# The first tile's k and q units on x times the norm's weights, its root multiplied in where the banks are emptied

## What is computed

```python
h = x * rsqrt(mean(x * x) + 1e-6) * g_pre_mix
z, q, k, v, glow, og = split(h @ w_in)
gk = log_sigmoid(glow @ w_gk2 + b_gk2) / 16
pool_out = pool_mixer(z)                 # causal window means, a map per group
gla_out  = gla_mixer(q, k, v, gk, og)    # gated linear attention, 4 heads
x = x + rmsnorm(concat(pool_out, gla_out) @ w_o)
x = x + rmsnorm(conv_ffn(rmsnorm(x)))
x = x + (p @ w_ple) * sigmoid(x @ w_ple_gate)
```

## Time and profile before

| | us |
|---|---|
| runs of the kernel before | 2514.07 (median), 2513.3, 2518.11 |
| the profiled execution, its own time | 2515.29 |
| its span, first to last instruction | 2513.5 |
| PE busy in the span | 2492.4 (99%) |
| DVE busy | 1542.4 (61%) |
| ACT busy | 1256.4 (50%) |
| POOL busy | 178.5 (7%) |
| mean granted clock of TensorE, share of full | 0.999 |

### The profile page before, as it was taken

The page is one execution under the profiler, slowest core; times in us unless marked ns, Lnnn a source line. Parts: engine busy times, 40 slices in busy tenths (PEclk is TensorE's granted clock), DMA queues, the critical chain, the costliest instruction groups (busy, mean ns, idle before and its releaser), DMA issues.

```text
span 2513.5 us, 40470 instructions
## 1 busy us (share of the span) xinstructions
PE 2492.4 (99%) x16216; PEld 2429.2 (97%) x16216; DVE 1542.4 (61%) x2479; ACT 1256.4 (50%) x1959; POOL 178.5 (7%) x508
## 2 busy tenths in 40 slices
PE   9999999999999999999999999999999999999999
PEld 8889999989999999999999999999999999999999
DVE  7668765556665554666545466654546664647865
ACT  5455554554444455544445544444545444546554
POOL 4201000100000010000001000000100000010000
PEclk9999999999999999999999999999999999999999
DMA  8555556554444656444465644446564444676665
GB/s 252 181 187 160 183 147 224 195 200 147 151 122 129 217 178 209 151 152 126 125 221 175 214 151 151 123 126 212 177 217 151 144 125 128 206 251 208 192 184 170
DMA packets 128250, 437.40 MB, mean 174 GB/s; under 512 B 13760, under 2 KB 23360, under 8 KB 127552
## 3 DMA queue, kind: packets, MB, share of 16 engines
q1 hardware_dynamic: 128064, 434.82, 54.2%
HBM read 403.48 MB, written 31.28 MB: 173 GB/s over the span
## 4 chain that ended last, share of the span: by engine, by line
PE 95%; DVE 2%; DMA 1%; ACT 1%; issue 0%; POOL 0%; SPq 0%; DVEq 0%; POOLq 0%; ACTq 0%
PE G L1682 29%; PE G L1683 28%; PE G L1684 28%; PE X L1728 2%; PE G L1966 1%; PE G L1967 1%; PE G L1968 1%; PE X L1786 1%; PE X L1678 1%; DMA kept_lo<-w_lo 1%; DVE w_lo L1164 0%; DMA stage<-in_w_up_units_dram 0%; PE X L1792 0%; PE X L1707 0%; PE X L1771 0%
## 5 line engine op out<-in xcount | busy, mean ns | idle before, releaser
L1682 PE MATMUL G<-h_hi,w_hi 128*128 128x384 f32 (+2 forms) x3072 | 997.9, 325 | 6.5 <-DVE w_lo L1164 3.3
L1683 PE MATMUL G<-h_hi,w_lo 128*128 128x384 f32 (+2 forms) x3072 | 988.0, 322 | 0.0
L1684 PE MATMUL G<-h_lo,w_hi 128*128 128x384 f32 (+2 forms) x3072 | 988.0, 322 | 0.0
L749 ACT ACTIVATE w_hi<-stage 128x1024 fp32r<-128x1024 f32 (+1 forms) x457 | 473.2, 1036 | 421.8 <-DMA stage<-in_w_up_units_dram 248.3
L1164 DVE TENSOR_TENSOR w_lo<-stage,w_hi 128x1024 fp32r<-128x1024 f32 (+1 forms) x457 | 546.0, 1195 | 138.8 <-ACT w_hi L749 137.9
L1682 PEld LDWEIGHTS G<-h_hi,w_hi 128*128 128x128 f32 x3072 | 579.6, 189 | 14.0 <-DVE w_lo L1164 4.3
L1683 PEld LDWEIGHTS G<-h_hi,w_lo 128*128 128x128 f32 x3072 | 579.6, 189 | 1.5
L1684 PEld LDWEIGHTS G<-h_lo,w_hi 128*128 128x128 f32 x3072 | 579.5, 189 | 0.0
L1682 PE MATMUL G<-y_hi,w_hi 128*128 128x384 f32 (+2 forms) x1056 | 342.6, 324 | 0.0
L1684 PE MATMUL G<-y_lo,w_hi 128*128 128x384 f32 (+2 forms) x1056 | 339.4, 321 | 0.0
L1683 PE MATMUL G<-y_hi,w_lo 128*128 128x384 f32 (+2 forms) x1056 | 339.3, 321 | 0.0
(11 more groups left out here) (220 smaller groups left out, 2703.9 us busy)
## 6 DMA issues: line engine op xcount, KB each, us to landing
stage<-in_w_up_units_dram SPq DMA_DIRECT2D x264, 512.0 KB, 3.6
w_lo<-kept_lo SPq DMA_DIRECT2D x145, 512.0 KB, 4.8
stage<-in_w_down_units_dram SPq DMA_DIRECT2D x96, 448.0 KB, 3.3
w_whole<-in_w_in_units_dram SPq DMA_DIRECT2D x72, 512.0 KB, 3.9
stage<-in_w_down_units_dram SPq DMA_DIRECT2D x48, 512.0 KB, 3.5
w_hi<-kept_hi SPq DMA_DIRECT2D x40, 512.0 KB, 3.6
w_whole<-in_w_gate_units_dram SPq DMA_DIRECT2D x33, 512.0 KB, 3.8
kept_lo<-w_lo SPq DMA_DIRECT2D x32, 512.0 KB, 5.1
```

Source lines behind the costliest of these rows:

```text
L749: act.activation(w_hi[s][:, 0:parts, :], whole[:, 0:parts, :], ACT.Copy).then_inc(hi_made, 1)
L1682: pe.matmul(ps[:, 0:w], l_hi, r_hi[:, 0:w], start=start, stop=False)
L1683: pe.matmul(ps[:, 0:w], l_lo, r_hi[:, 0:w], start=False, stop=False)
L1684: return pe.matmul(ps[:, 0:w], l_hi, r_lo[:, 0:w], start=False, stop=stop)
```

## The change

In tile 0 the units `in` 0 to 3 and `glow` no longer use h. ACT makes `raw_hi`, the high part of x times the gain of the norm, as the quarters of x land, and DVE the rest, `raw_lo`. PE multiplies with these. The missing factor, the root `rms_x` of each token, is multiplied in where a result is read from PSUM, now by DVE: `evacuate_raw` for k and q, `norm_glow` for glow. For glow, which multiplies x itself, DVE first makes `w_glow_raw`, the small weights times the gain. The squares are no longer added on DVE: PE takes each of the 8 with its own `ones_sum`, between the products of units 0 and 1. h is still needed from v on: `norm_x`, `h_split` and `h_rest` of its 8 blocks now run as `two_h`, two blocks at each of the units 1 to 4. `values` waits for each block. SP issues const and unit 0 after the first quarter of x, the states after unit 3, and `S_s` before unit `in` 9. POOL clears the operands after unit `in` 3 (`raw_hi`, `raw_lo` lie in their place). The 20 matmuls on ones go.

```diff
+            load_first_x(0)
+            sp.dma_start(const[:, 0:C_GK], packed[:, 0:C_GK]).then_inc(const_loaded, 16)
             load_unit(0)
+            for a in range(1, KD // 2):
+                load_first_x(a)
             load_unit(1)
...
-                if t:
-                    pool.wait_ge(*tick((t - 1, "down", 3 * KD - 1)))
+                pool.wait_ge(*tick((t - 1, "down", 3 * KD - 1) if t else (0, "in", 3)))
...
             act.preload_act_table_set(LN_EXP)
-            for m in range(KD):
-                square_x(0, m)
+            for m in range(0, KD, 2):
+                raw_split(m)
+                raw_split(m + 1)
+                if m in (0, 4):
+                    make_hi(m // 4)
+                for k in (m, m + 1):
+                    act.wait_ge(first_x_loaded[k // 2], 16)
+                    first_square(xr[0][:, k, :], sq_x, total_x, k, x_squared, first_x_taken)
             act.wait_ge(built, 4)
             root_x(0)
-            make_hi(0)
-            for m in range(KD):
-                h_split(0, m)
-                if m == 1:
-                    make_hi(1)
-            make_hi(2)
-            copy_glow(0)
...
+            def evacuate_raw(m):
+                w = width(0)
+                b, _n = out_bank((0, "in", m))
+                dve.wait_ge(*x_rooted.at(0))
+                dve.wait_ge(*tick((0, "in", m)))
+                if m < 2:
+                    last = dve.tensor_tensor(kT[:, m, 0:w], G[b][:, 0:w], rms_x[:, 0:w], ALU.mult)
...
+            def two_h(m):
+                norm_x(0, m)
+                norm_x(0, m + 1)
+                h_rest(0, m)
+                h_rest(0, m + 1)
...
-            for m in range(1, KD):
-                add_x(0, m)
-            dve.wait_ge(const_loaded, 16)
-            norm_x(0, 0)
-            for m in range(1, KD + 1):
-                if m < KD:
-                    norm_x(0, m)
-                if m in (1, 3):
-                    make_lo(m // 2)
-                h_rest(0, m - 1)
+            for m in range(0, KD, 2):
+                raw_rest(m)
+                raw_rest(m + 1)
+                if m in (0, 4):
+                    make_lo(m // 4)
+                if m == 2:
+                    scale_glow_weights()
...
                 make_lo(n + 1)
                 if kind == "in":
+                    if t == 0 and m == 0:
+                        norm_glow()
                     if t == 0 and m == 1:
+                        evacuate_raw(0)
+                        least_gate(0)
                         make_lo(n + 2)
+                        two_h(0)
+                        dve.wait_ge(built, 9)
+                        sum_gate(0)
+                        evacuate_raw(1)
+                    if t == 0 and 2 <= m <= 4:
+                        if m > 2:
+                            evacuate_raw(m - 1)
+                        two_h(2 * m - 2)
...
+                        if t == 0:
+                            pe.wait_ge(*h_lo_made.at(0, k))
                         pe.matmul(ps, h_hi[:, k, some], hi[:, k % 2, :], start=k == 0, stop=False)
...
-            sum_x(0)
-            units_by_block(0, 2, h_hi, h_lo, h_lo_made.at, 2, warm=20)
-            pe.wait_ge(tables_loaded, 16)
-            make_glow(0)
+            units_by_block(0, 2, raw_hi, raw_lo, raw_ready, 2, first_x_block)
             make_gk(0)
```

More of the change, by code:

```diff
@@ L231, in hybrid_layer @@
         g_past = own("g_past", [P, 2, NF])
+        w_glow_raw = own("w_glow_raw", [P, KD, 32])
         g_state = own("g_state", [P, NSEQ, 2, NF])
@@ L544, in store_y, with load_first_x @@
                 y_stored.did(sp.dma_start(of_tile(y_feat, t, KD)[:, first:last, :], y_out[:, first:last, 0:width(t)]), t, a)
-            def load_first_x():
-                for a in range(KD // 2):
-                    two = slice(2 * a, 2 * a + 2)
-                    sp.dma_start(xr[0][:, two, 0:width(0)], of_tile(x_feat, 0, KD)[:, two, :]).then_inc(first_x_loaded[a], 16)
-            load_first_x()
+            def load_first_x(a):
+                two = slice(2 * a, 2 * a + 2)
+                sp.dma_start(xr[0][:, two, 0:width(0)], of_tile(x_feat, 0, KD)[:, two, :]).then_inc(first_x_loaded[a], 16)
+            load_first_x(0)
+            sp.dma_start(const[:, 0:C_GK], packed[:, 0:C_GK]).then_inc(const_loaded, 16)
             load_unit(0)
-            sp.dma_start(const[:, 0:C_GK], packed[:, 0:C_GK]).then_inc(const_loaded, 16)
+            for a in range(1, KD // 2):
+                load_first_x(a)
             load_unit(1)
@@ L556, in _ @@
             load_unit(2)
+            for n in range(3, SLOTS):
+                load_unit(n)
             sp.dma_start(z_in[:, :], z_feat[:, :]).then_inc(states_loaded, 16)
             sp.dma_start(g_state[:, :, :, :], g_feat[:, :, :, :]).then_inc(states_loaded, 16)
-            for n in range(3, SLOTS):
-                load_unit(n)
-            for b in range(2):
-                sg = state_gla[0].rearrange("b (d h) k v -> h k b d v", h=2)[b]
-                sp.dma_start(S_s[head_rows(b), :, :, :], sg).then_inc(s_loaded, 16)
             for n in range(SLOTS, len(UNITS)):
                 t, kind, m = UNITS[n]
+                if (kind, m) == ("in", 9) and t == 0:
+                    for b in range(2):
+                        sg = state_gla[0].rearrange("b (d h) k v -> h k b d v", h=2)[b]
+                        sp.dma_start(S_s[head_rows(b), :, :, :], sg).then_inc(s_loaded, 16)
                 if (kind, m) == ("down", 20) and t < LAST:
@@ L813, in evacuate_in @@
                         copy_v(t, c)
+                    return
+                if t == 0 and m < 4:
                     return
@@ L1024, in _ @@
                         decay_gate(0)
+                    if t == 0 and 1 <= m <= 4:
+                        h_split(0, 2 * m - 2)
+                        h_split(0, 2 * m - 1)
                     if m == 1 and t:
@@ L1698, in make_glow @@
             def make_glow(t):
-                take(3, glow_copied.at(t))
+                take(3, glow_copied.at(t) if t else (first_glow_copied, 1))
                 for k in range(KD):
@@ L1705, in glow_block @@
                 j = k % 4
[L1706 to L1708 removed]
+                if t:
+                    pe.wait_ge(*h_made.at(t, k))
+                else:
+                    pe.wait_ge(glow_weights_scaled, 1)
+                    pe.wait_ge(first_x_loaded[k // 2], 16)
+                return pe.matmul(X[3][32 * j:32 * j + 32, 0:width(t)], (w_glow if t else w_glow_raw)[:, k, :],
+                                 (h_full if t else xr[0])[:, k, 0:width(t)], start=k < 4, stop=k >= 4)
             def make_gk(t):
[L1711 removed]
+                pe.wait_ge(*glow_copied.at(t) if t else (first_glow_copied, 1))
                 for d in range(2):
@@ L1896, in sum_d, with first_x_block, raw_ready @@
                 d_summed.did(ones_sum(X[4], total, t), t)
+            def first_x_block(k):
+                if k == 0:
+                    take(2, x_rooted.at(0))
+                first_sum(X[2], sq_x, total_x, k, x_squared, first_x_taken)
+                if k == KD - 1:
+                    make_glow(0)
+            def raw_ready(t, k):
+                return raw_lo_made, k + 1
             def halves_ready(n):
@@ L2031, in _ @@
                         values(n, v_banks)
+                    elif t == 0 and 2 <= m < 4:
+                        whole_unit(n, raw_hi, raw_lo)
                     elif t or m >= 2:
```

57 lines of the change are left out of this document (40 added, 17 removed).

## The result

The changed kernel takes 2525.66 us (median of six runs, 2522.06 to 2526.51). Against the runs of the kernel before on the same chip the ratio is 1.0038, with a 95% interval from 1.0028 to 1.0048: 9.6 us slower, between 7 and 12. One of the six runs of before that stood beside them took 11286.87 us and is left out. Forecast were 2520.2 us, 5.9 over before, and the range ended at 2525.5. The direction and the first of the two forecast waits came out as written; the loss is 3.7 us larger, and the rest of this text says where that lies.

The account below looks back on a forecast made before the run. PE, busy for 99% of the span, was taken to bind, with DVE's queue as full between 27 and 34 us. Head -0.5 and two waits +6.4 gave +5.9 us, forecast 2520.2 us, range 2515.0 to 2525.5.

Parts of the forecast that it names:

- the two forecast waits: PE in the v units: 3.9 us for unit 4's low half, then 2.5 us for bank 0; together +6.4 us.
- The bound: Whole span: PE is busy for 99%, so a delay put on it anywhere is paid at the end.
- The head: Start up to gk: first product near 9.2, gk at 24.9 against 25.39; -0.5 us, between 0.9 won and 1.5 lost.
- The tables: Load that glow's weight scaling on DVE waits for: landed at 11.8 us; a microsecond later in the head's loss case.
- PE's wait for unit 1: Head: PE idle about 2.7 us before unit 1's first product, until DVE ends its low half at 14.4.
- The cost of a sum: Head, on PE: each sum of squares between products takes 0.58 us; seven more are 4.1 us.
- PE isn't held for unit 1: Part of the faster rival (chance 0.07): tables by 9.5 and the square not waiting give 2.7 us more.
- DVE behind gk: DVE's queue from `least_gate` at 27.3 takes 9.9 us; unit 4 ready at 37.2, PE wants it at 33.3, waits 3.9.
- the idle stretch: DVE before `least_gate`: the 3.71 us idle before 26.64 stay idle, since glow and the root come late.
- The second wait: Unit 4's third piece: PE waits 2.5 us until DVE has read q out of bank 0, free at 42.4.
- The clock: Rival, chance 0.2: the clock falls in the new idle stretches; one gives +7.6 to +9.3 us, two give 2527.
- Later tiles are as they were: Everything behind the first tile: no change; from unit 5 on nothing gives the loss back.

Follow-up runs that it names:

- e4: The kernel before with 50 matmuls on ones in place of 20 ahead of its first product, a pure delay of PE: 2520.66 us, ratio 1.0020.
- e2: The changed kernel with unit 1 split one step sooner on ACT and DVE, ahead of the scaling of glow's weights: 2521.84 us, ratio 1.0024.
- e5: The kernel before with eight more DVE operations, their result unused, ahead of the split of unit 4: 2523.81 us, ratio 1.0030.
- e1: The changed kernel with unit 4's split and the readouts of banks 2 and 3 ahead of the gate sums, four h blocks behind: 2528.0 us, ratio 1.0049.
- e6: The changed kernel with unit 1 split sooner, two sums per step, glow at the sixth, h blocks in DVE's idle time: 2517.48 us, ratio 1.0004.
- e3: The changed kernel with 14 matmuls on ones on PE in the stall ahead of unit 4: 2526.26 us, ratio 1.0041.
- e8: The kernel before with 50 matmuls on ones instead of 20 and eight added DVE operations ahead of unit 4's split: 2527.93 us, ratio 1.0043.
- e7: The kernel before with its squares summed by eight pairs of PE matmuls, not DVE's adds; 14 matmuls on ones, not 28: 2517.15 us, ratio 1.0006.

## Why the prediction was right or wrong

**The bound.** Right: a delay of PE in the start is paid at the end. e4 shows it by itself.

**The head.** Forecast was a gain of 0.5 us with a loss of 1.5 as its worse end; gk began at 26.21 instead of 24.9, 0.8 later than before. This is the first term that was mis-sized. The tables landed at 13.2, not 11.8, as the row at 13.21 shows, so the split of unit 1 ended at 15.7 and not 14.4. From there to gk the forecast was 10.5 us and the trace has 15.75 to 26.21, so the late tables are the whole miss. The first product came at 10.33, not 9.2, since the 28 matmuls on ones took 9.46 us and not the 8.14 of the earlier trace rows, with no edit to them; that shortened PE's wait for unit 1, which was 2.80 (2.7 forecast), and cost nothing. The tables a microsecond late stood in the bounds, so gk lies within them, in their worse half; the late first product did not. The cost of a sum was right: a product with a sum behind it takes 0.98 us to the next start (11.13 to 12.11 on that timeline), one without 0.44, so 0.54 for the sum, 0.58 forecast. e2 takes the wait away and wins 2.9 us at gk, as the rival "PE isn't held for unit 1" had priced it (2.7).

**DVE behind gk.** Right, and the best supported step. From gk's start to the ready low half of unit 4 I worked out 12.3 us; the trace has 38.41 - 26.21 = 12.2. PE's wait was forecast at 3.9 us and was 3.69. e5 makes the same stall with DVE's load alone, e1 shows one order behind gk that only moves it, and e6 that it goes when the root comes sooner and the work moves ahead of gk, into the 6.38 us in which DVE had nothing. What the prediction hadn't drawn is that conclusion: it named the idle stretch (then 3.71 us, said to "stay idle") and did not say that it is the root, held back by sums placed one to a product, that keeps DVE from it.

**The second wait.** Forecast 2.5 us, measured 0.44, and the reason is not a shorter queue: bank 0 was read out 4.8 us behind the split (5.2 forecast), but PE came to it 1.6 us later, at half clock. With the clock held up, e3 measured 1.76. The two together, second wait and slow clock, cost unit 4 2.1 us over its usual 4.1. So +6.4 for the two waits was nearly right as a sum, but partly by luck, since the half clock took the place of most of the second wait: PE is 6.95 us late at unit 5, 0.8 of it the head's and 6.1 the waits', against a forecast of 5.9. The difference is the head, 1.3 us worse than forecast, less 0.3.

**The clock.** I had it as a rival with 0.2, adding 1.7 to 3.4 us to the forecast. It fell behind the stall of 3.69 us and stayed whole around that of 2.80; the same wait for unit 1 kept it in e3 (2.52 us) and brought it down in e1 (2.92 us). The Trainium skill, "TensorE: Matmul & The Clock Gate", Part 1, says that an idle TensorE goes back to half its clock; the trace agrees for the longer stall, in e2, e5 and e8 too, and the shorter one shows that not every wait does it. But at that place it cost nothing that e3 can show, where another queue hid it, and 1.7 us in e5, where none did. I was wrong to price it without asking what PE would have waited for next.

**What was left out, and the step that failed.** The prediction adds up the loss as far as unit 5 and puts all that follows at nothing: "Later tiles are as they were". This is the term that failed. In the trace PE is 6.9 us late at unit 8 and 10.6 at the end, so this term measured 3.6 us; the runs' 9.6 less the 6.9 leave 2.7. Behind unit 8 both kernels have the same matmuls, so the two traces can be laid against each other, matmul by matmul, for how late the changed one is:

| time in the changed trace, us | us late at its end | what happens there |
|---|---|---|
| 62 to 70 | 6.95 | nothing |
| 70 to 80 | 8.45 | half clock, 72 to 75.5 |
| 80 to 112 | 6.91 | half clock in both kernels, 3.4 us here and 6.8 us before |
| 112 to 120 | 8.95 | half clock, 113 to 120 |
| 120 to 157 | 10.47 | clock whole; longer waits |
| 157 to 200 | 11.33 | half clock, 157.5 to 164.3; before has a wait of 1.89 us here, the changed kernel none |
| 200 to 600 | 11.35 | half clock, 560 to 563.6 |
| 600 to the end | 10.59 | a wait of 0.5 us at 2331 that only before has |

How the first such stretch looks in the changed kernel, on PE's timeline:

```profile
71.44 0.66 PE L1790 MATMUL X<-queries,opnd 64*128 64x64 f32 x8
72.03 0.38 PE L1795 MATMUL X<-queries,opnd 64*64 64x32 f32 x4
72.34 0.63 PE L1740 MATMUL G<-h_hi,w_hi 128*128 128x320 f32 x1
72.77 0.47 PE L1741 MATMUL G<-h_hi,w_lo 128*128 128x320 f32 x1
```

Nobody waits here. A run of small matmuls ends, the clock falls to half in it, and the products behind take 0.47 us instead of 0.31. It is the pattern of the earlier trace rows, in a place where before kept its clock, and it costs 1.5 us. Not every stretch costs as much. Rows of the changed kernel from 134 us on, then those of before:

```profile
134.71 1.13 PE L1911 MATMUL X<-stage,const 128*128 128x128 f32 x8 [1.44 <-DMA stage<-in_w_o_units_dram]
...
159.91 4.57 PE L2003 MATMUL G<-ones 128*128 128x128 f32 x20
...
569.28 0.45 PE L1740 MATMUL G<-h_hi,w_hi 128*128 128x384 f32 x1 [0.51 <-DVE w_lo L1178]
```

```profile
125.12 1.13 PE L1847 MATMUL X<-stage,const 128*128 128x128 f32 x8 [0.64 <-DMA stage<-in_w_o_units_dram]
...
148.34 2.50 PE L1929 MATMUL G<-ones 128*128 128x128 f32 x20
152.73 0.42 PE L1682 MATMUL G<-h_hi,w_hi 128*128 128x320 f32 x1 [1.89 <-DVE h_lo L1406]
...
557.92 0.44 PE L1682 MATMUL G<-h_hi,w_hi 128*128 128x384 f32 x1 [1.40 <-DVE w_lo L1164]
```

The stretch at 157 falls mostly on matmuls on ones, which take 4.57 us instead of 2.50 and eat a wait that before has behind them. The one at 560 is given back in full, since PE waits for DVE behind it in any case (0.51 us instead of 1.40). And between 120 and 157 us the changed kernel loses 1.5 to 1.7 us with its clock whole, 1.1 of it in two longer waits for loads (1.9 us together against 0.8) and 0.6 in a longer one for DVE. So of the 3.6 us some 2.9 came by the end of stretches at half clock, net of that of before and of what waits gave back, and 0.8 in waits at whole clock.

The mean clock of the changed kernel's runs was 0.9953, that of before 0.9978, and all six of its runs lay between 0.994 and 0.997. What 0.001 is worth differs with the set of before's runs that one asks: 1.5 us between the medians at 0.999 and 0.997 in one (seven and eight runs), 1.1 in another (six and five). An estimate from these, 0.0025 at 1.1 to 1.5 us for each 0.001, is 2.8 to 3.8 us, which fits the 2.7 us that the runs leave and proves nothing by itself.

**Open** is what decides where the clock falls. A shift of PE alone doesn't bring more stretches (e4: 0.9974). With a DVE stall (e5: 0.9963) and with both (e8) the profiled execution has several, but e6 and e7, whose time is that of before, have one and two more than before in their traces too. No run here took the late stretches away by themselves, and of the longer waits for loads no run tells the cause.

**The range** ended 0.2 us too low, since it took the fall of the clock as a case instead of the forecast, put everything behind unit 5 at nothing, and had the tables' lateness as a bound, not as likely. That the sum at unit 5 came within 1 us is in part luck, as said above.

## What to carry to other kernels

When work is moved from before a root to behind it, ask where the engine that gets it is idle: here the same operations cost 8 us in one order and nothing in another (e6), and that order became possible because the sums, and so the root, were done sooner. Moving them within the full stretch (e1) moved the wait and took none away. Where PE is busy for 99% of the span, each microsecond of stall in the start was paid at the end, and the half clock behind a stall cost more only where nothing else was late beside it.

## What was unexpected of the hardware

- The same first matmuls on ones, with no edit, took 8.14 us in one execution and 9.46 in another (9.03 in e4). PE's records begin at 7 in a microsecond and go on at 11; the step comes near 5 us in the first and near 8 us in the second. The granted clock reads 1.00 in all these windows, so that the clock makes the step is read from the pace, not from that column. The Trainium skill, "TensorE: Matmul & The Clock Gate", Part 1, says that the number of slow matmuls at the start varies from run to run; the trace agrees. Where nothing else is waited for at the start, this is a microsecond either way.
- Runs of one kernel differ by 3 us with their mean clock (seven at 0.999 against eight at 0.997), and profiled executions of kernels of the same time have one to three stretches at half clock near 95 to 160 us.
- What a stretch at half clock costs depends on what lies in it and behind it: 1.5 us for the 3.4 us at 72, 0.9 us for the 6.8 us at 157, where matmuls on ones and a wait took up the rest, and nothing for the 3.4 us at 560, where PE waits for DVE next.
- The load of the tables, 512 KB, landed 1.4 us later than the 11.8 worked out from the earlier trace rows, though it was issued at the same time (4.29 us); no run here tells why.
